# Depthwise convolution on TensorE: four taps per product instead of two, with the shifted copies issued by ScalarE, the diagonals built by VectorE, and a reworked opening

## The chip, the cores and the metric

One Trainium2 chip, one of its cores. The metric is the device time of one execution in microseconds (us). TensorE is the matrix engine (PE in the profile), VectorE is DVE, ScalarE is ACT, GpSimd is POOL, and SyncE is SP, which here only issues transfers and waits. Everything is float32. Most matrix products are made as three products of float32r halves (a high part and the rest), which keep float32 precision.

## The reference

Input x has 512 tokens of 1024 features. A first block has two layers: a pool mixer (mean over the last 2, 4, 8 or 16 tokens, minus the token, times a small matrix) and sliding-window attention, each with an RMS norm before it and a gated feed-forward behind it (2816 wide, with a 3-tap convolution over time). A second block follows:

```python
def conformer_conv(x, w_in, b_in, conv_w, conv_b, ln_g, ln_b, w_out, b_out):
    a, g = jnp.split(x @ w_in + b_in, 2, axis=-1)
    h = a * jax.nn.sigmoid(g)
    h = conv_general_dilated(h, conv_w, padding=30 on the left, groups=1024) + conv_b   # 31 taps
    h = jax.nn.silu(layer_norm(h, ln_g, ln_b))
    return h @ w_out + b_out
x = x + conformer_conv(rms_norm(x), ...)
x = x + square(relu(rms_norm(x) @ w1)) @ w2          # 4096 wide
```

The change touches the pool mixer (the opening), the first pair of each feed-forward, and the 31-tap convolution.

## The kernel before, in words

Features lie on the 128 partitions, in `C` = 8 chunks; tokens are the 512 columns. Every engine has its own program, and they wait on semaphores. Weights come in units of 128 x 1024 through four slots: SP loads `raw`, ScalarE copies the high part to `whi` (`split_hi`), VectorE subtracts it into `wlo` (`split_lo`), and TensorE runs a chain of 8 x 3 products (`three`, L594 to L596). A slot of `raw` is loaded again once it has been split.

*The opening.* The pool weights are scaled by the norm's gain (`weigh_pooled`, one half each on ScalarE and VectorE), `project_pooled` multiplies x with them (L683), `token_sums` adds the squares, and `window_mean` (L706, L709) applies the windows as banded matrices: a product with zeros opens each PSUM bank, and four products of 129 to 143 columns add into it. The bands (`near`, L530 and L533) are made by GpSimd from the identity in the constants `cst`, then weighted by VectorE (`mix`) and by both engines with 1/rms (`mixed`). `bias_residual` (ScalarE, L1079) adds the pool bias to `res`; `add_pooled` (L1530) and `prepare` (L958, L1347) then make the first feed-forward's inputs `xh` and `xl`, whose products begin in `first_chains`.

*The convolution stage.* For each chunk c the `ain` weights are applied (two chains), `gated` (VectorE, L1730) writes `hc` with 30 zero columns ahead of its 512, and the 31 taps of the chunk are shared out by hand:

- `PE_TAPS[c]` taps on TensorE (`convolve`, L867). SP copies `hc` into `shifted` (`shift_hc`, L480): partitions 0 to 63 hold 64 channels, 64 to 127 the same channels one token later, so one product of 128 rows with a two-diagonal matrix `dg` does two taps of 64 channels. There are two such column groups. ScalarE makes `dg` by scaling an identity (`diagonals`, L1230).
- `POOL_TAPS[c]` taps as ScalarE's scaled copies (`products`, L1244) which GpSimd adds up (L580).
- The others on VectorE (`own_tap`, L1686 and L1689, in the same step; `late_tap`, L1699, one step later, into the PSUM bank of `convolve`, so after `conv_done`). `collect` (L1707, L1712) adds the three parts into `hv`.

For ten units of `ain` and four of `aout` the low part is made otherwise: ScalarE writes the negated high part (`negate_high`, L1253) and a transfer issued by GpSimd adds the weights to it (L568). `statistics` (L877, L879) sums `hv` and its square over the features in two column groups; the layer norm and the output projection follow.

The order in every queue is fixed by the code. SP's is: two weight loads, then the four copies of a chunk, which wait for that chunk's `hc`.

Of the kernel before, what the change touches and what calls it, by code (L numbers as in the profile page):

```python
# [28 lines left out]
P = 128  # L29
D = 1024  # L30
T = 512
# [20 lines left out]
LAST_DIAGS = 5  # L52
HC = 3
LAST_GATED = 14
LOW_AT = {6: (0, 8), 7: (0, 10), 8: (1, 5), 9: (1, 7), 10: (2, 5), 11: (2, 7), 12: (3, 6), 13: (3, 8), 14: (4, 6),
          15: (4, 8), 16: (5, 7), 17: (7, 3), 18: (7, 6), 19: (7, 6)}
# [3 lines left out]
WARM = 10  # L60
# [105 lines left out]
def build(nc, xT, vec_in, cst_in, w_in, out):  # L166
# [3 lines left out]
    with ExitStack() as ctx:  # L170
# [14 lines left out]
        with ExitStack() as own:  # L185
# [3 lines left out]
            near = sb("near", [P, 5, PAD + P + PAD], F32, own)  # L189
            mix = sb("mix", [P, 2, 4, P + PAD], F32, own)  # L190
            mixed = sb("mixed", [P, NBLK, 4, P + PAD], F32, own)
            zero = sb("zero", [P, T], F32R, own)
# [5 lines left out]
        with ExitStack() as own:  # L198
# [7 lines left out]
            pair_w = sb("pair_w", [P, SHIFTS, C * TAPS], F32, own)  # L206
            pair_id = sb("pair_id", [P, GROUP], F32, own)
# [3 lines left out]
        with ExitStack() as own:  # L211
            hv = sb("hv", [P, C, T], F32, own)
            hc = sb("hc", [P, HC, TAPS - 1 + T], F32, own)
            dg = sb("dg", [P, DIAGS, max(PE_TAPS) // SHIFTS, SHIFTS, GROUP], F32, own)
            tapped = sb("tapped", [P, PARTS, T], F32, own)
            shifted = sb("shifted", [P, 2, SHIFTS, max(PE_TAPS) - SHIFTS + T], F32, own)
# [50 lines left out]
        near_steps = sem("near_steps")  # L267
        mix_steps = sem("mix_steps")
# [99 lines left out]
        on = slice(PAD, PAD + P + PAD)  # L368

# [59 lines left out]
        def _(sp):  # L429
# [31 lines left out]
            def load_pairs():  # L461

                w, i = VEC["conv_w"], CST_ID
                for s in range(SHIFTS):
                    rows = slice(s * GROUP, (s + 1) * GROUP)
                    sp.dma_start(pair_id[rows, :], cst_in[0:GROUP, i:i + GROUP]).then_inc(pairs_loaded, 16)
                    for g in range(SHIFTS):
                        n = C * TAPS - s
                        sp.dma_start(pair_w[rows, g, 0:n], vec_in[g * GROUP:(g + 1) * GROUP, w + s:w + s + n])\
                            .then_inc(pairs_loaded, 16)  # L470

            def shift_hc(c):

                n = PE_TAPS[c] - SHIFTS + T
                sp.wait_ge(hc_ready, c + 2)
                if c >= 2:
                    sp.wait_ge(conv_done, c - 1)
                for g in range(SHIFTS):
                    for s in range(SHIFTS):
                        sp.dma_start(shifted[s * GROUP:(s + 1) * GROUP, c % 2, g, 0:n],  # L480
                                     hc[g * GROUP:(g + 1) * GROUP, c % HC, s:s + n]).then_inc(hc_shifted[c % 2], 16)

            def load_conv_stage():

                ain, aout = ph["ain"], ph["aout"]
                shifts = {2 * c + KT - 2: c for c in range(C)}
                for n in range(ain.units + aout.units):
                    p, e = (ain, n) if n < ain.units else (aout, n - ain.units)
                    load(p, e // SLOTS, e % SLOTS)
                    if n in shifts:  # L490
                        shift_hc(shifts[n])

            for p in order:
                if p.name == "ffn0_up0":
                    sp.wait_ge(x_in[3], 16)
                if p.name == "pool":
                    load(p, 0, 0)
                    sp.dma_start(res[:, 0:2, 2 * P:T], xT[:, 0:2, 2 * P:T]).then_inc(x_in[0], 16)
                    for k in range(1, SLOTS):
                        load(p, 0, k)  # L500
                    continue
# [17 lines left out]
        def _(pool):  # L519


            pool.wait_ge(setup, 1)
            pool.wait_ge(cst_loaded, 16)
# [6 lines left out]
            nc.gpsimd.tensor_copy(near[:, 0, PAD:PAD + P], ident).then_inc(near_steps, 1)  # L530
            for g in range(4):
                pool.wait_ge(near_steps, g + 2)
                nc.gpsimd.tensor_tensor(near[:, g + 1, on], near[:, g, on],  # L533
# [1365 lines left out]
```

## Time and profile before

| | |
|---|---|
| median of 3 runs | 1448.52 us (1448.52 to 1449.33) |
| profiled execution, its own time | 1448.29 us |
| its span, first to last instruction | 1446.5 us |
| granted TensorE clock over the span | 1.00 |
| instructions in the trace | 19954 |

A span is counted from the first instruction. Line numbers are those of the kernel before. A row of the timeline merges neighbouring instructions of one kind and begins with its start and its length in us; in brackets stands the engine's idle time before it and what ended that. A float32 product is two records in the trace, a float32r product one.

### The profile page before, as it was taken

The page shows a single profiled execution, that of the slowest core. Times are in us where ns is not written, and L with a number is a line of the kernel's source. Part 1 is how long each engine was busy: PE and PEld are TensorE (multiplying, and loading weights), DVE is VectorE, ACT ScalarE, POOL GpSimd, SP SyncE. Part 2 cuts the span into 40 slices and gives each one's busy share as a digit, 9 for nine tenths or more (in the row PEclk, how much of TensorE's full clock was granted, in tenths as well). Part 3 has the DMA queues.
Part 4 walks back from the last instruction along what each step waited for, and adds up shares of the span by engine and source line. Part 5 has one row for each costly group of instructions (what it writes and reads, how often), then busy time and mean ns, then how long its engine had stood idle before and what let it go on. Part 6 is the DMA issues. An engine that isn't in the chain of part 4 may idle for free.

```text
span 1446.5 us, 19954 instructions
## 1 busy us (share of the span) xinstructions
PE 1437.2 (99%) x6828; PEld 1172.1 (81%) x6828; DVE 921.2 (64%) x1339; ACT 637.3 (44%) x994; POOL 204.8 (14%) x162
## 2 busy tenths in 40 slices
PE   9999999999999999999999999999999999999999
PEld 8788888888887898888888888766588888888887
DVE  7877773573645667777754755899988653544532
ACT  7444442342546675444422434798754321222210
POOL 4000000000302232000000003599511000000000
PEclk9999999999999999999999999999999999999999
DMA  5223223222322112232232232387613332222321
GB/s 191 88 99 104 87 102 116 73 102 91 121 90 71 30 60 81 96 108 94 91 125 75 88 108 81 101 186 179 161 45 102 116 101 89 100 102 88 102 94 51
DMA packets 44413, 144.34 MB, mean 100 GB/s; under 512 B 5184, under 2 KB 6208, under 8 KB 44352
## 3 DMA queue, kind: packets, MB, share of 16 engines
q1 hardware_dynamic: 41200, 133.79, 28.0%
q0 software_dynamic: 2016, 7.34, 2.8%
q10 hardware_dynamic: 1136, 2.42, 0.4%
q8 instruction: 35, 0.57, 0.2%
q14 instruction: 26, 0.21, 0.0%
HBM read 137.19 MB, written 2.10 MB: 96 GB/s over the span
## 4 chain that ended last, share of the span: by engine, by line
PE 94%; DVE 2%; ACT 1%; DMA 1%; issue 1%; POOL 1%; SPq 0%; ACTq 0%; DVEq 0%; POOLq 0%
PE bank L594 29%; PE bank L595 29%; PE bank L596 29%; PE bank L867 2%; PE bank L742 1%; PE bank L770 1%; PE bank L755 1%; DVE bank L1689 1%; PE bank L877 0%; DMA cst<-cst_in 0%; DMA shifted<-hc 0%; PE bank L922 0%; PE bank L923 0%; PE bank L635 0%; PE bank L926 0%
## 5 line engine op out<-in xcount | busy, mean ns | idle before, releaser
L594 PE MATMUL bank<-xh,whi 128*128 128x512 f32 x1184 | 464.9, 393 | 0.8 <-DVE wlo L1340 0.6
L596 PE MATMUL bank<-xh,wlo 128*128 128x512 f32 x1184 | 460.9, 389 | 0.0
L595 PE MATMUL bank<-xl,whi 128*128 128x512 f32 x1184 | 460.8, 389 | 0.0
L945 ACT ACTIVATE whi<-raw 128x1024 fp32r<-128x1024 f32 x244 | 255.8, 1050 | 238.7 <-PE bank L596 236.0
L1340 DVE TENSOR_TENSOR wlo<-raw,whi 128x1024 fp32r<-128x1024 f32 x230 | 288.0, 1252 | 43.8 <-ACT whi L945 35.9
L594 PEld LDWEIGHTS bank<-xh,whi 128*128 128x128 f32 x1184 | 222.2, 188 | 55.4 <-issue 7.1
L595 PEld LDWEIGHTS bank<-xl,whi 128*128 128x128 f32 x1184 | 222.3, 188 | 46.6 <-issue 1.2
L596 PEld LDWEIGHTS bank<-xh,wlo 128*128 128x128 f32 x1184 | 222.3, 188 | 46.4
L594 PE MATMUL bank<-ahi,whi 128*128 128x512 f32 x608 | 236.5, 389 | 0.0
L595 PE MATMUL bank<-alo,whi 128*128 128x512 f32 x608 | 236.5, 389 | 0.0
L596 PE MATMUL bank<-ahi,wlo 128*128 128x512 f32 x608 | 236.5, 389 | 0.0
L1361 DVE TENSOR_TENSOR res<-bank,res 128x512 f32 (+1 forms) x80 | 55.3, 691 | 202.6 <-PE bank L596 202.6
L545 POOL TENSOR_TENSOR ssum<-ssum,sq 128x512 f32<-128x512 f32 x32 | 47.7, 1490 | 733.8 <-ACT sq L965 403.2
L1412 DVE SCALAR_TENSOR_TENSOR tmp<-u,vec,tmp 128x512 f32<-128x512 f32 x176 | 124.2, 747 | 31.8 <-ACT tmp L1004 31.8
L596 PEld LDWEIGHTS bank<-ahi,wlo 128*128 128x128 f32 x608 | 114.1, 188 | 23.8
L594 PEld LDWEIGHTS bank<-ahi,whi 128*128 128x128 f32 x608 | 114.1, 188 | 23.7
L595 PEld LDWEIGHTS bank<-alo,whi 128*128 128x128 f32 x608 | 114.1, 188 | 23.5
L1004 ACT ACTIVATE tmp<-u,vec 128x512 f32<-128x512 f32 x88 | 71.6, 814 | 125.3 <-DVE u L1407 125.3
L1407 DVE TENSOR_TENSOR u<-bank,rinv 128x512 f32<-128x512 f32 x88 | 59.5, 685 | 63.8 <-PE bank L596 63.8
L580 POOL TENSOR_TENSOR prod<-prod,tapped 128x512 f32<-128x512 f32 x56 | 77.3, 1380 | 7.0 <-POOL prod L580 0.5
L1026 ACT ACTIVATE ahi<-tmp 128x512 f32 (+1 forms) x32 | 20.2, 632 | 121.6 <-DVE tmp L1437 121.6
L1008 ACT ACTIVATE gate<-tmp 128x512 f32<-128x512 f32 x44 | 27.9, 633 | 96.3 <-DVE tmp L1412 96.3
(191 smaller groups left out, 1344.6 us busy)
## 6 DMA issues: line engine op xcount, KB each, us to landing
raw<-w_ffn_up SPq DMA_DIRECT2D x88, 512.0 KB, 3.3
raw<-w_ffn_down SPq DMA_DIRECT2D x32, 512.0 KB, 3.2
raw<-w_mlp_up SPq DMA_DIRECT2D x32, 512.0 KB, 3.2
raw<-w_mlp_down SPq DMA_DIRECT2D x32, 512.0 KB, 3.2
raw<-w_ain SPq DMA_DIRECT2D x16, 512.0 KB, 3.4
raw<-w_ffn_down SPq DMA_DIRECT2D x16, 384.0 KB, 3.0
raw<-w_qkv SPq DMA_DIRECT2D x12, 512.0 KB, 3.2
wlo<-w_ain POOLq DMA_DIRECT2D x10, 512.0 KB, 7.3
```

The lines of the kernel that those rows point to most:

```text
L545: nc.gpsimd.tensor_tensor(ssum[:, which, :], ssum[:, which, :], x, ALU.add)\
L580: nc.gpsimd.tensor_tensor(prod[:, c % 2, :], a, tapped[:, (made + k) % PARTS, :], ALU.add)\
L594: nc.tensor.matmul(out_, hi, mh, start=first, stop=False)
L595: nc.tensor.matmul(out_, hi, ml, start=False, stop=False)
L596: return nc.tensor.matmul(out_, lo, mh, start=False, stop=last)
L867: mm = nc.tensor.matmul(bank[6 + b][g * GROUP:(g + 1) * GROUP, :], dg[:, c % DIAGS, q, g, :], shifted[:, b, g, SHIFTS * q:SHIFTS * q + T], ...
L945: nc.scalar.activation(whi[:, s, 0:tiles * P], raw[:, s, 0:tiles * P], ACT.Copy)\
L1004: nc.scalar.activation(tmp[:, k, :], u[:, k, 2:2 + T], ACT.Identity, scale=col(vec, par + 2), bias=col(vec, par + 3))\
L1340: V.tensor_tensor(wlo[:, s, 0:tiles * P], raw[:, s, 0:tiles * P], whi[:, s, 0:tiles * P].bitcast(F32), ALU.subtract).then_inc(lo_done, 1)
L1361: V.tensor_tensor(row(res, c), acc[k][:], row(res, c), ALU.add).then_inc(acc_free, 1)
L1407: V.tensor_tensor(u[:, k, 2:2 + T], acc[k][:], rinv[:], ALU.mult).then_inc(acc_free, 1)
L1412: V.scalar_tensor_tensor(tmp[:, k, :], u[:, k, shift:shift + T], col(vec, par + 4 * j + shift), tmp[:, k, :], op0=ALU.mult, op1=ALU.add).t ...
```

## The change

- `convolve` works with `SHIFTS[c]` taps per product: four for chunks 0 to 6 (four column groups of 32 channels, each row group of `shifted` one token later), two for chunk 7. `PE_TAPS` goes from 68 taps in all to 86, `POOL_TAPS` from 72 to 65, and VectorE's from 108 to 97. `DIAGS` (buffers of `dg`) goes from 3 to 2.
- `shift_hc` moves from SP to ScalarE, ahead of the chunk's `products`. Each of its transfers (one per column group) reads the overlapping windows of its channels and writes all 128 partitions. It is four transfers a chunk, as before, each with twice the rows (two for chunk 7).
- `diagonals` moves from ScalarE, 68 small copies, to VectorE, one product of two broadcast operands per chunk, behind `gated`. `load_pairs` brings its operands in 22 transfers, before 6.
- In step 6 the last `gated` comes after `collect`, no longer between taps.
- `statistics` uses four column groups of 32, each over half of the tokens.
- The opening: no product with zeros; `near` is made by GpSimd from ones with a memset and six selects, with no wait for `cst`; the residual bias goes to GpSimd; 8 warm-up products, before 10; the orders of splits and of the window weights change; x's last quarter and the tail of `vec` are issued by SP.
- The first pair of a feed-forward: ScalarE's and VectorE's second weight split come ahead of the taps.

```diff
-PE_TAPS = (8, 6, 6, 4, 6, 6, 14, 18)
-SHIFTS = 2
-GROUP = P // SHIFTS
+PE_TAPS = (8, 8, 8, 8, 8, 12, 20, 14)
+SHIFTS = (4, 4, 4, 4, 4, 4, 4, 2)
+GROUP = tuple(P // s for s in SHIFTS)
+ROUNDS = tuple(n // s for n, s in zip(PE_TAPS, SHIFTS))
-DIAGS = 3
-POOL_TAPS = (11, 10, 9, 9, 9, 9, 8, 7)
-LATE_TAPS = (0, 6, 8, 11, 11, 12, 4, 0)
-LATE_START = (2, 2, 2, 0, 0, 0, 0, 4)
+DIAGS = 2
+POOL_TAPS = (10, 9, 9, 8, 8, 8, 7, 6)
+LATE_TAPS = (2, 4, 6, 9, 12, 9, 0, 0)
+LATE_START = (2, 2, 2, 0, 0, 0, 0, 0)
-WARM = 10
+WARM = 8
...
-            def shift_hc(c):
-
-                n = PE_TAPS[c] - SHIFTS + T
-                sp.wait_ge(hc_ready, c + 2)
-                if c >= 2:
-                    sp.wait_ge(conv_done, c - 1)
-                for g in range(SHIFTS):
-                    for s in range(SHIFTS):
-                        sp.dma_start(shifted[s * GROUP:(s + 1) * GROUP, c % 2, g, 0:n],
-                                     hc[g * GROUP:(g + 1) * GROUP, c % HC, s:s + n]).then_inc(hc_shifted[c % 2], 16)
+                for shifts, (lo, hi) in SPREAD.items():
+                    group, n = P // shifts, PAIR_TAPS[shifts]
...
+                    for s in range(shifts):
+                        for g in range(shifts):
+                            src = vec_in[g * group:(g + 1) * group, w:w + C * TAPS].rearrange("p (c k) -> p c k", c=C)
+                            sp.dma_start(pair_w[shifts][s:P:shifts, g], src[:, lo:hi, s:s + n]).then_inc(pairs_loaded, 16)
...
+            def band(g, in_, base, sign, op):
+
+                nc.gpsimd.affine_select(near[:, g, :], near[:, in_, :], [[sign, P + PAD]], op, 0.0, base=base,
+                                        channel_multiplier=-sign).then_inc(near_steps, 1)
+
+            nc.gpsimd.memset(near[:, 4, :], 1.0).then_inc(near_steps, 1)
+            pool.wait_ge(near_steps, 1)
+            band(0, 4, 0, 1, ALU.is_equal)
+            band(3, 4, 0, 1, ALU.is_ge)
+            pool.wait_ge(near_steps, 3)
+            for g in (1, 2, 4, 3):
+                band(g, 3, WINDOWS[g - 1] - 1, -1, ALU.is_ge)
...
+            pool.wait_ge(setup, 2)
+            pool.wait_ge(squared, C)
+            for c in range(C):
+                pool.wait_ge(chain_done, 2 * (c // 2) + 2)
+                nc.gpsimd.tensor_scalar(res[:, c, :], res[:, c, :], col(pbs, c), None, ALU.add).then_inc(res_biased, 1)
...
-                nc.tensor.matmul(bank[BAND_BANKS[c]][:], zero[:, 0:P], zero[:], start=True, stop=False)
...
+                for q in range(ROUNDS[c]):
+                    for g in range(SHIFTS[c]):
+                        rows, at = slice(g * group, (g + 1) * group), SHIFTS[c] * q
+                        mm = nc.tensor.matmul(bank[6 + b][rows, :], dg[:, c % DIAGS, q, rows],
+                                              shifted[:, b, g, at:at + T],
+                                              start=(q == 0), stop=(q == ROUNDS[c] - 1))
...
-                nc.tensor.matmul(norm[0][0:GROUP, :], ones[:, 0:GROUP], hv[:, c, :],
-                                 start=(c == 0), stop=(c == C - 1))
-                nc.tensor.matmul(norm[0][GROUP:P, :], ones[:, 0:GROUP], sq[:, c % 2, :],
-                                 start=(c == 0), stop=(c == C - 1)).then_inc(stats_done, 1)
+                for j, x in enumerate((hv[:, c, :], sq[:, c % 2, :])):
+                    for h in range(2):
+                        rows, at = slice((2 * j + h) * QUADRANT, (2 * j + h + 1) * QUADRANT), slice(h * T // 2, (h + 1) * T // 2)
+                        mm = nc.tensor.matmul(norm[0][rows, at], ones[:, 0:QUADRANT], x[:, at],
+                                              start=(c == 0), stop=(c == C - 1))
...
+            def shift_hc(c):
+
+                n, group = PE_TAPS[c] - SHIFTS[c] + T, GROUP[c]
+                if c >= 2:
+                    act.wait_ge(conv_done, c - 1)
+                for g in range(SHIFTS[c]):
+                    window = hc[g * group:(g + 1) * group, c % HC, 0:n]
+                    taps = bass.AP(window.tensor, window.offset, [window.ap[0], (1, SHIFTS[c]), (1, n)])
+                    act.dma_start(shifted[:, c % 2, g, 0:n], taps).then_inc(hc_shifted[c % 2], 16)
...
                 act.wait_ge(hc_ready, c + 2)
+                shift_hc(c)
                 products(c, range(2))
...
+            def diagonals(c):
+
+                if c >= DIAGS:
+                    dve.wait_ge(conv_done, c - DIAGS + 1)
+                if c == 0:
+                    dve.wait_ge(pairs_loaded, 16 * sum(s * s + 1 for s in SPREAD))
+                shifts, rounds, group = SHIFTS[c], ROUNDS[c], GROUP[c]
+                shape = [P, rounds, shifts, group]
+                w = pair_w[shifts][:, :, c - SPREAD[shifts][0], 0:shifts * (rounds - 1) + 1:shifts]
+                V.tensor_tensor(dg[:, c % DIAGS, 0:rounds].rearrange("p q (g n) -> p q g n", g=shifts),
+                                pair_id[shifts][:].rearrange("p (q g n) -> p q g n", q=1, g=1).broadcast_to(shape),
+                                w.rearrange("p g (q n) -> p q g n", n=1).broadcast_to(shape), ALU.mult)\
+                    .then_inc(diag_ready, 1)
```

## Rows read from the trace of the kernel before

**Rows 1.** The page's first part: busy time and share of the span.

```profile
PE 1437.2 (99%) x6828; PEld 1172.1 (81%) x6828; DVE 921.2 (64%) x1339; ACT 637.3 (44%) x994; POOL 204.8 (14%) x162
```

**Rows 2.** Chain of waits, opening: start us, us, what.

```profile
2.23 6.83 DMA cst<-cst_in
...
14.74 0.77 POOL near L533
```

**Rows 3.** Timeline of the opening, TensorE and VectorE.

```profile
7.09 10.59 PE L683 MATMUL bank<-wg,res 128*128 128x256 f32 x48
...
21.94 0.50 PE L706 MATMUL bank<-zero 128*128 128x512 f32 x1
...
23.09 0.47 PE L706 MATMUL bank<-zero 128*128 128x512 f32 x1
...
37.02 0.19 PEld L594 LDWEIGHTS bank<-xh,whi 128*128 128x128 f32 x1 [0.62 <-DVE xl L1347]
...
41.24 2.30 DVE L1340 TENSOR_TENSOR wlo<-raw,whi 128x1024 fp32r<-128x1024 f32 x1
...
55.43 0.50 PE L594 MATMUL bank<-xh,whi 128*128 128x512 f32 x1 [0.62 <-DVE wlo L1340]
```

**Rows 4.** Chain of waits, convolution stage.

```profile
944.90 6.61 DMA shifted<-hc
951.55 2.80 PE bank L867 x12
...
965.46 2.73 PE bank L867 x12
...
980.14 1.87 PE bank L867 x8
...
1030.38 7.73 PE bank L867 x36
1038.11 0.42 PE bank L877
```

**Rows 5.** Timeline of VectorE, convolution stage.

```profile
929.43 0.75 DVE L1730 SCALAR_TENSOR_TENSOR hc<-bank,vec,gate 128x512 f32<-128x512 f32 x1 [0.19 <-ACT gate L1266]
...
942.33 0.75 DVE L1730 SCALAR_TENSOR_TENSOR hc<-bank,vec,gate 128x512 f32<-128x512 f32 x1
...
944.91 5.50 DVE L1689 SCALAR_TENSOR_TENSOR bank<-hc,vec,bank 128x512 f32<-128x512 f32 x7
...
959.57 0.75 DVE L1689 SCALAR_TENSOR_TENSOR bank<-hc,vec,bank 128x512 f32<-128x512 f32 x1
960.23 0.75 DVE L1699 SCALAR_TENSOR_TENSOR bank<-hc,vec,bank 128x512 f32<-128x512 f32 x1
...
974.74 0.69 DVE L1720 TENSOR_TENSOR tmp<-bank,rinv 128x512 f32<-128x512 f32 x1 [1.04 <-PE bank L596]
...
1039.97 3.34 DVE L1774 RECIPROCAL r<-r 128x512 f32<-128x512 f32 x1
```

**Rows 6.** Groups of VectorE, 925 to 1042: busy us, mean ns, idle before.

```profile
L1707 DVE TENSOR_TENSOR hv<-prod,hv 128x512 f32<-128x512 f32 x8 | 7.9, 993 | 0.4 <-POOL prod L580 0.4
```

**Rows 7.** The page's costliest groups, same columns.

```profile
L1340 DVE TENSOR_TENSOR wlo<-raw,whi 128x1024 fp32r<-128x1024 f32 x230 | 288.0, 1252 | 43.8 <-ACT whi L945 35.9
```

**Rows 8.** Groups of ScalarE, 925 to 1042.

```profile
L1244 ACT ACTIVATE tapped<-hc,vec 128x512 f32<-128x512 f32 x72 | 46.6, 720 | 7.8 <-DVE hc L1730 7.0 <-POOL prod L580 0.8
L1230 ACT ACTIVATE dg<-pair_id,pair_w 128x64 f32<-128x64 f32 x68 | 17.1, 335 | 0.0
```

**Rows 9.** Stretches: length, busy per engine, PEclk, DMA share, GB/s.

```profile
943.00:1013.00 70.00, 69.23 (x302) 46.90 (x301) 67.15 (x96) 62.26 (x111) 65.39 (x54) 1.00 0.79 189
1026.00:1030.00 4.00, 4.00 (x22) 1.35 (x20) 3.86 (x7) 4.00 (x8) 0.76 (x1) 1.00 0.56 135
```

**Rows 10.** The tile `shifted`: issue ns min/median/max, and landing.

```profile
L480 SPq DMA_DIRECT2D shifted<-hc x32: 467/597/2171, 930.2 to 1027.3; - x32
...
DMA to landing us min/median/max: 2.2/2.8/6.6
```

More of the change, by code:

```diff
@@ L529, in _ @@
             nc.gpsimd.tensor_tensor(square_of(0), square_of(0), square_of(2), ALU.add).then_inc(early_summed, 1)
[L530 to L533, printed above, removed]
-                                        near[:, g, PAD - (1 << g):2 * PAD + P - (1 << g)], ALU.add)\
-                    .then_inc(near_steps, 1)
+            pool.wait_ge(setup, 2)
[3 more added lines that the diff above has]
+                nc.gpsimd.tensor_scalar(res[:, c, :], res[:, c, :], col(pbs, c), None, ALU.add).then_inc(res_biased, 1)
             def add_squares(name):
@@ L997, in step @@
                             k = 2 * b + j
-                            split_hi(p.unit, i, k + AHEAD)
-                            if first and isinstance(i, int) and i == 0 and k == 0:
+                            opening = first and isinstance(i, int) and i == 0
+                            if not (opening and k == 1):
+                                split_hi(p.unit, i, k + AHEAD)
+                            if opening and k == 0:
                                 root(first)
+                                split_hi(p.unit, i, 1 + AHEAD)
                             par = VEC["glu"] + ((layer * FF_PAIRS + q0) * 2 + k) * 4 + 16 * i
@@ L1218, in _ @@
             p = ph["ain"]
-            def diagonals(c, part=0, parts=1):
-                if c >= DIAGS and part == 0:
-                    act.wait_ge(conv_done, c - DIAGS + 1)
-                if c == 0:
-                    act.wait_ge(pairs_loaded, 16 * SHIFTS * (SHIFTS + 1))
-                pairs = PE_TAPS[c] // SHIFTS
-                for q in range(part * pairs // parts, (part + 1) * pairs // parts):
-                    e = c * TAPS + SHIFTS * q
-                    for g in range(SHIFTS):
-                        last = nc.scalar.activation(dg[:, c % DIAGS, q, g, :], pair_id[:], ACT.Copy,
-                                                    scale=pair_w[:, g, e:e + 1])
-                if part == parts - 1:
-                    last.then_inc(diag_ready, 1)
             def products(c, ks):
@@ L1414, in step @@
                                                        op0=ALU.mult, op1=ALU.add).then_inc(done, 1)
-                        split_lo(p.unit, i, 2 * b + 1 + AHEAD)
+                        if not opening:
+                            split_lo(p.unit, i, 2 * b + 1 + AHEAD)
                         dve.wait_ge(gate_ready, pair + 1)
@@ L1531, in add_pooled @@
                                        op0=ALU.mult, op1=ALU.add).then_inc(pooled, 1)
-            for g in range(4):
-                weigh_pooled(g)
+            weigh_pooled(0)
+            window_weights()
+            weigh_pooled(1)
+            first_window_weights()
+            weigh_pooled(2)
+            weigh_pooled(3)
             evict_pooled(0)
@@ L1543, in _ @@
             V.tensor_tensor(square_of(4), square_of(4), square_of(0), ALU.add).then_inc(all_summed, 1)
[L1544 to L1545 removed]
+            for m in range(C):
+                for half in range(2):
+                    h = C * (m // REP) + REP * half + m % REP
+                    made = V.memset(qs[HD * half:HD * (half + 1), m:m + 1], HD ** -0.5 / SLOPE[h])
+            made.then_inc(q_scales, 1)
             dve.wait_ge(rms_ready, 1)
@@ L1756, in _ @@
                 gate_at = next((n for n in range(rounds) if issued[n] >= GATE_AT), rounds - 1)
-                gated_at = next((n for n in range(rounds) if issued[n] >= LAST_GATED), rounds - 1)
                 for n in range(rounds):
```

164 lines of the change are left out of this document (67 added, 97 removed).

## Prediction

> **What bounds the kernel now.** I read the page first. TensorE is busy for 99% of the span [rows 1], so only what shortens TensorE's queue, or a wait on it, can move the time. The chain of waits says where that is not so. In the opening it runs through the constant load, GpSimd's band matrices and ScalarE [rows 2], and in the convolution stage through one transfer of `shifted` [rows 4]. From 60 us to 916 us, and after the layer norm, TensorE is fed without gaps and the diff touches nothing there.
>
> The timeline of the opening [rows 3] shows TensorE working back to back: 48 records of projection from 7.09, the last 16 after the token sums, then eight window products from 21.94 at a pitch of about 1.15 (the second begins at 23.09). Two idle spots of 0.62 us follow, at 37.02 and 55.43.
>
> In the convolution stage the table of stretches [rows 9] has four engines nearly full over 70 us: TensorE 69.2, VectorE 67.2, GpSimd 65.4, ScalarE 62.3, and the DMA engines at 0.79. A step of this stage is one chunk of 128 channels. VectorE goes from its first `hc` at 929.43 to the reciprocal at 1039.97, 110 us, and waits in that time for little but TensorE, 1.04 us at 974.74 being the longest [rows 5]. So TensorE and VectorE end together, and taking work from TensorE alone gives nothing: the slower of the two sets the gain.
>
> **The opening, part by part.** *Zero products.* Each window product began with a 512-column float32r product of zeros. A float32r product of this width takes about 0.23 us of the queue (48 of them between 954.35 and 965.46 [rows 4]), and eight go: 8 x 0.22 = -1.7 us. *Start.* Ten warm-up products become eight and VectorE no longer waits for ScalarE's half of the pool weights. TensorE starts about 0.5 us earlier, but two fewer warm products may leave the first projection at the slower pace; bounds 0 and -0.5, I take -0.3. *Band matrices.* GpSimd makes them with seven operations before the constants land at 9.06, in place of five after [rows 2]. Selects do not occur in the trace; the nearest operation took 0.77 us, seven are 5.4 us, done before the first squares. Bounds: nothing, or, at twice that they end near 11 us and hold VectorE's second pool weight back by about 1.5 us. I take nothing. The 16 memsets of `q_scale` move into slack. *Residual bias.* Eight ScalarE operations go to GpSimd, which idled there, so ScalarE and VectorE can feed `xl` faster, two VectorE operations of 0.75 a chunk [rows 5] where TensorE needs 6 x 0.23 = 1.4. Of the 0.62 at 37.02 a part goes: -0.3. *First pair of the feed-forward.* A weight split moves ahead of the taps, and the 0.62 at 55.43 goes: -0.6. Against it, the split of unit 6 now comes after all eight `prepare` calls, and such a split took 2.30 us beside GpSimd's adds at 41.24 [rows 3]. It may be late by 0 to 0.8: +0.4. Sum: -1.7 - 0.3 - 0.3 - 0.6 + 0.4 = -2.5, bounds -3.3 and -0.5.
>
> **The convolution stage on TensorE.** A pair of taps was four records (two column groups, two passes). The chain has 7.73 us for 36 records and 1.87 for eight [rows 4]: 0.86 to 0.93 a pair, although the records last 0.6 each, so the two groups run side by side. There were 34 pairs. There are now 18 rounds of four groups and 7 of two, 25 in all. If four groups run side by side as two do, 9 rounds x 0.88 = -7.9 us. Statistics: two passes of 0.42 a chunk [rows 4] become four quadrants over half the columns, 0.42 in all: 8 x 0.43 = -3.4. Together -11.3. The dear end: if only two groups ran at once, a four-group round costs 1.75, and the stage gets 18 x 0.88 - 7.9 = +7.9 in place of -7.9. I take the cheap end, as two groups overlap fully in the rows.
>
> The Trainium skill bears on this (TensorE: Matmul & The Clock Gate, Part 3, table of measured speedups): three column tiles gave 2.38x and four row tiles 3.07x, not 3x and 4x. An estimate by that rule, 4 x 0.88 / 3.07 = 1.15 us a round, would make the TensorE saving smaller by 18 x 0.27 = 4.9 us. The trace has no four-group product.
>
> **The stage on VectorE.** Taps left to it fall from 108 to 97 (own 56 to 55, late 52 to 42). A tap that follows one on the same accumulator costs 5.50 / 7 = 0.786; one that alternates, 960.23 - 959.57 = 0.66 [rows 5]. Writing out the order gives 56 and 52 before, 59 and 38 after: 78.3 to 71.4, -6.9 us. Added are eight `diagonals`, 3200 columns in all. A split of 1024 columns takes 1252 ns [rows 7] and an evict of 512 some 0.69 [rows 5], so about 1.1 ns a column and 0.13 each, of which 0.08 lies over the operation before: +3.9. They have two SBUF inputs, like L1707, whose mean is 993 ns [rows 6] where the same width takes 0.69 when nothing stands in its way. Bounds 0 and 8 x 0.3 = 2.4; I take +1.2. Its waits for TensorE and GpSimd, about 1.7, go: -1.7. Sum: -6.9 + 3.9 + 1.2 - 1.7 = -3.5, bounds -4.7 and -2.3. The wait of `diagonals(c)` for `conv_done` of chunk c-2 is met a whole step earlier, so only two buffers cost nothing.
>
> **ScalarE and GpSimd.** ScalarE loses the 68 diagonal copies, 17.1 us, and 7 of 72 products, 4.5 us [rows 8]. It gains 30 DMA issues; on SP they took 597 ns each [rows 10], 18 us. Net -3.6. But the issues stand ahead of the products: at each chunk about 2.4 us in which ScalarE feeds GpSimd nothing. GpSimd has 7 of 64 adds fewer and catches up. Queued behind them are also the next sigmoid and two weight splits; by my ledger ScalarE finishes a step between 2 us before and 1 us after the next `hc`. I add nothing. SP is freed of the `hc` wait, and loads weights no later. 22 small pair loads (before: 6) take some 13 us of SP ahead of the attention weights; a slot is asked for when its last content is split, some three units of 5.5 us before the next is needed (two units fill 954.35 to 965.46 [rows 4]), which covers them.
>
> **The transfer.** Its bytes double: four transfers of 128 rows by 516 columns a chunk, where there were four of 64 rows. Before, the last of four landed 8.4 us after `hc` in a busy step (943.09 to 951.51 [rows 4, 5]), and single landings ranged from 2.2 to 6.6 [rows 10]. Chunk 7's four, alone on the engines, used a share of 0.56 over 4 us [rows 9], so each chunk adds 2.2 us of all 16. That makes about 10.5 us after `hc`. TensorE comes to the product 8 to 11 us after `hc`, so it waits 1 to 2 us at chunks 1 and 2 (it waited for the transfer at chunk 1 before too), then hardly. VectorE meets it at the first late tap, 13 us after `hc`, where 12.4 is the last landing that costs nothing. I take +0.5.
>
> **Sum.** Stage end: VectorE -3.5, transfers +0.5, and after the last `hv` one statistics chunk half as long, -0.4: -3.4. With the opening's -2.5: -5.9 us. The profiled execution took 1448.29 us around its span of 1446.5; it becomes 1442.4. The median of the runs shown is 1448.52, 0.2 higher, which makes 1442.6; I say 1442.5. What a measurement can tell from no change is about 0.2%, 2.9 us.
>
> **The rivals.** *TensorE sets the pace after all.* If `diagonals` meet no blocking and the tap counts let VectorE keep up, the stage gains up to TensorE's 11.3 less the wait at chunk 1, say 8, and the time is 1448.3 - 2.5 - 8 = 1438. Against it stands VectorE's ledger.
>
> *The transfer is late: the one that ends slower.* The table has the DMA engines at 0.79 over 70 us [rows 9], about 11.2 us of a 14.2 us step. With 2.2 more in a step of 13.2 they are at 1.01. If landings slip to H+15, where H is the chunk's `hc`, the late taps of four or five steps each start 2.6 us late: +11.7, that is 1448.3 - 5.9 + 11.7 = 1454. At H+13.7 the gain is gone. For it: the share itself, and that late taps begin with no delay from chunk 3 on. Against it: that share counts weight loads which are short when alone. The Trainium skill (DMA: Bandwidth & Descriptors, decision table) says transfers issued from different engines use the same 16 DMA engines, so moving the issue to ScalarE saves only issue time; it would speak for this rival.
>
> *Four groups do not run together.* TensorE's stage is then 7.9 - 3.4 = 4.5 us longer and it is the bound: 1448.3 - 2.5 + 4.5 = 1450. A half-way speedup would still leave TensorE level with VectorE, near 1444.
>
> *The stage does nothing.* Blocking and ScalarE's late products eat the 3.4, only the opening is left: 1446.
>
> **How the numbers follow.** Forecast (1440 to 1445) 0.55; TensorE pace, 1438, 0.15; stage does nothing, 1446, 0.15; late transfer 0.10; groups not together 0.05. Faster by over 0.2% (under 1445.6): 0.55 + 0.15 + a part of the third, 0.08 = 0.78. Slower: most of the late transfers, 0.07, and a little of the groups, 0.01 = 0.08. The same: 0.14. The range reaches from the TensorE pace to just above no change: 1437 to 1448.5; the forecast's own is 1440 to 1445.
>
> **What would show it.** Opening: no zero products, window pitch near 0.92, the first feed-forward product near 29 us and not 31.1, no wait at 55. Stage: eight records of L867 in four groups take about 0.9 a round; the span from first `hc` to the reciprocal is 107, not 110.5; the share of DMA above 0.9; `diagonals` of two rounds at 0.4 us, longer when beside a GpSimd add. I am wrong if L867 waits for `shifted` after chunk 2, if a four-group round takes over 1.1 us, or if ScalarE's products start later than 3 us after `hc`.

## The result, and the profile after

The changed kernel takes 1471.15 us (median of 4 runs, 1465.93 to 1472.09) where the kernel before took 1448.53 beside it: a ratio of 1.0144, with the interval 1.0132 to 1.0157. It is 22.6 us slower; 5.9 us faster was forecast, and the range ended at 1448.5. The profiled execution is the fastest of the four, 1465.93 us around a span of 1464.1, so 17.6 of the 22.6 us can be looked for in its trace.

The page's first part, and the rows of the 40 slices for TensorE's busy time and its clock:

```profile
PE 1432.6 (98%) x6884; PEld 1168.0 (80%) x6884; DVE 925.2 (63%) x1334; ACT 612.9 (42%) x911; POOL 209.9 (14%) x165
...
PE   9999999999999999999999999978899999999999
...
PEclk9999999999999999999999999989999999999999
```

TensorE is busy 4.6 us less than before [rows 1] and yet the span is 17.6 us longer: it now waits, and one slice of its clock falls. Both are in the convolution stage. The stretches of that stage (the same 70 us as in [rows 9], and the two worst steps in it; the last columns are granted clock, DMA share and GB/s):

```profile
943.00:1013.00 70.00, 54.58 (x268) 36.65 (x266) 55.03 (x76) 45.90 (x64) 52.71 (x45) 0.88 0.84 207
943.00:963.00 20.00, 9.09 (x40) 6.50 (x42) 16.98 (x23) 13.10 (x18) 16.30 (x15) 0.78 0.88 223
963.00:983.00 20.00, 20.00 (x100) 13.05 (x93) 13.64 (x19) 10.34 (x15) 13.97 (x12) 0.88 0.82 203
```

No engine is full any more: TensorE 54.6 of 70 us against 69.2, VectorE 55.0 against 67.2, ScalarE 45.9 against 62.3, while DMA went from 0.79 to 0.84. TensorE waits for something that no engine computes, and the others wait behind it. The tile `shifted` names it (issue in ns; then who waited for the tile, us and times; then the landings):

```profile
L1256 ACTq DMA_DIRECT2D shifted<-hc x30: 550/646/3471, 928.7 to 1041.8; - x30
...
  PE bank L869: 23.0, 4
  DVE bank L1689: 8.7, 2
  DVE hv L1716: 3.6, 1
...
DMA to landing us min/median/max: 3.7/7.5/15.5
```

Against [rows 10] the median landing went from 2.8 to 7.5 us and the longest from 6.6 to 15.5. TensorE waits 23.0 us in four places: 2.09 at chunk 0, 10.88 at chunk 1, 4.51 at chunk 4 and 5.54 at chunk 7. The largest, at chunk 1, on ScalarE and on TensorE (timeline):

```profile
942.08 1.06 ACT L1232 ACTIVATE wlo<-whi 128x1024 fp32r<-128x1024 f32 x1
943.04 1.04 ACT L950 ACTIVATE whi<-raw 128x1024 fp32r<-128x1024 f32 x1
944.12 1.07 ACT L1232 ACTIVATE wlo<-whi 128x1024 fp32r<-128x1024 f32 x1
944.12 6.13 ACTq L1256 DMA_DIRECT2D shifted<-hc  x4
950.30 5.71 ACT L1223 ACTIVATE tapped<-hc,vec 128x512 f32<-128x512 f32 x9 [5.12 <-issue]
...
951.05 0.39 PE L598 MATMUL bank<-xh,wlo 128*128 128x512 f32 x1
962.32 3.64 PE L869 MATMUL bank<-shifted,dg 128*32 128x512 f32 x16 [10.88 <-DMA shifted<-hc]
...
977.89 1.92 PE L869 MATMUL bank<-shifted,dg 128*32 128x512 f32 x16
...
1009.28 3.37 PE L869 MATMUL bank<-shifted,dg 128*32 128x512 f32 x16 [4.51 <-DMA shifted<-hc]
```

`hc` of chunk 1 was written at 941.87. ScalarE was still in the weight splits and negations of the step before, so the first copy was issued at 944.12; the four issues held ScalarE until 950.3; the product began at 962.32, 20.4 us after `hc`. Between the issues of the copies, two more kinds of transfer start (GpSimd's and SP's rows of the same timeline), GpSimd's accumulating weight transfers and SP's weight loads:

```profile
944.50 1.04 POOL L570 DMA_DIRECT2D wlo<-w_ain  x1
...
948.25 0.87 POOL L570 DMA_DIRECT2D wlo<-w_ain  x1
...
945.67 5.03 SPq L448 DMA_DIRECT2D raw<-w_ain  x3
```

The first two copies landed 3.8 and 7.8 us after their issue, the last two 13.7 and 15.5. The three weight loads (512 KB each) were issued before or within 0.8 us of the last copy, and landed after 12.8 to 15.2 us.

The 16 records at 962.32 take 3.64 us and the 16 at 1009.28, behind a wait of 4.51, take 3.37; the same 16 at 977.89, with no wait ahead, take 1.92. The granted clock stands at 0.78 in the 20 us up to 963: from 955 to 966 it is 0.50, so the clock fell while TensorE was idle, and it ran at the lower of its two levels (1.2 GHz) for some products behind that. That is a second cost of a wait, on top of the wait. Not every wait has it: with SP issuing (next section) the 16 records behind waits of 2.28 and 1.95 us took 1.93 and 1.92.

The opening, TensorE in the changed kernel, then the rows of the kernel before that answer to the last three:

```profile
6.20 7.17 PE L686 MATMUL bank<-wg,res 128*128 128x256 f32 x32 [1.10 <-DMA res<-xT]
14.25 3.69 PE L686 MATMUL bank<-wg,res 128*128 128x256 f32 x16 [0.87 <-DVE zT L1480]
...
22.23 7.47 PE L711 MATMUL bank<-mixed,zT 128*128 128x129 f32 x64
29.45 0.48 PE L596 MATMUL bank<-xh,whi 128*128 128x512 f32 x1
...
42.38 1.02 PE L637 MATMUL bank<-ssum,ones 128*128 128x512 f32 x2
...
918.83 1.88 PE L637 MATMUL bank<-ssum,ones 128*128 128x512 f32 x4
```

```profile
31.11 0.48 PE L594 MATMUL bank<-xh,whi 128*128 128x512 f32 x1
...
42.87 1.02 PE L635 MATMUL bank<-ssum,ones 128*128 128x512 f32 x2
...
920.29 1.88 PE L635 MATMUL bank<-ssum,ones 128*128 128x512 f32 x4
```

The eight windows take 7.47 us, 0.93 each where the pitch was 1.15 [rows 3], and the first feed-forward product comes 1.66 us earlier. By the token sums at 42.4 only 0.5 of that is left. There is no wait at 55 us any more, and at 919 the lead is 1.46 us.

### The profile page after: what moved, and what is told of

Its sections match the earlier page's. It is cut to its first block and busy times, and to the rows that moved or that the text cites. A ratio compares the mean times of both kernels' runs of the same rounds, so it can differ in the third digit from the quotient of the medians.

```text
span 1464.1 us, 19991 instructions
## 1 busy us (share of the span) xinstructions
PE 1432.6 (98%) x6884; PEld 1168.0 (80%) x6884; DVE 925.2 (63%) x1334; ACT 612.9 (42%) x911; POOL 209.9 (14%) x165
## 5 line engine op out<-in xcount | busy, mean ns | idle before, releaser
L582 POOL TENSOR_TENSOR prod<-prod,tapped 128x512 f32<-128x512 f32 x49 | 67.2, 1372 | 5.6
```

What stands on the lines that cost most here:

```text
L582: nc.gpsimd.tensor_tensor(prod[:, c % 2, :], a, tapped[:, (made + k) % PARTS, :], ALU.add)\
```

## Where the copies are issued

**Issued by SP, all else as changed.**

```diff
+                    if n in shifts:            # in SP's weight loop, the old place
+                        shift_hc(shifts[n])    # four overlapping copies, sp.dma_start
...
-                shift_hc(c)                    # on ScalarE, ahead of products
```

> The changed kernel with shift_hc back on SP, at the place where the kernel before had it (after two weight loads, waiting there for hc). Bytes, pattern and taps are those of the change. Theory 1 (the doubled bytes keep the DMA engines full, whoever issues): still slow, 1462 to 1472 us, single landings of shifted 7 to 12 us. Theory 2 (the place on ScalarE: behind two splits and two negations, and ScalarE held for 4 to 6 us by the issues): back to 1440 to 1446 us, landings up to 7 us. Both in part: 1450 to 1460 us.

Measured 1451.26 us, ratio 1.0016 (1.0006 to 1.0026). So 19.9 us of the 22.6 come with the place of the issue. The tile `shifted` in this version:

```profile
L484 SPq DMA_DIRECT2D shifted<-hc x30: 548/634/2844, 928.2 to 1029.1; - x30
...
  PE bank L883: 11.8, 4
...
DMA to landing us min/median/max: 3.6/5.3/11.6
```

It is still no gain: 11.8 us of waits stay. (Over 943 to 1013 the DMA engines' mean share is 0.95 in this version and 0.84 in the changed kernel, which is 20 us slower: the mean share alone does not say which copies are late.)

**Issued by ScalarE, but ahead of the last splits and negations of the step before** (two of each ahead of chunk 1, one of each for chunks 2 to 6).

```diff
+                    act.wait_ge(hc_ready, c + 3)
+                    shift_hc(c + 1)
                     for e in range(2 * (c + AHEAD) + (c > 0), ...):
                         split_hi(p.unit, 0, e)
                         negate_high(e)
```

> The changed kernel, ScalarE still issues the copies, but those of chunks 1 to 6 are issued ahead of the weight splits and negations that end the step before, as soon as hc is there. If it is the place in ScalarE's queue (first issue of chunk 1 was 2.3 us after hc, behind splits) that makes them late: waits for shifted fall by some 2 us a chunk, 1458-1466. If it is the issues' own length on a full queue and the bytes: 1469-1473, because issues still take 3 to 6 us and what stands behind them (now the next splits) is late by as much. If the held splits starve TensorE: slower than 1473.

Measured 1459.31, ratio 1.0074 (1.0057 to 1.0091): 11.8 us come back by position alone. ScalarE at chunk 1:

```profile
942.12 4.48 ACTq L1256 DMA_DIRECT2D shifted<-hc  x4
946.70 1.07 ACT L950 ACTIVATE whi<-raw 128x1024 fp32r<-128x1024 f32 x1 [5.40 <-PE bank L598]
947.80 1.06 ACT L1232 ACTIVATE wlo<-whi 128x1024 fp32r<-128x1024 f32 x1
```

The copies are issued at `hc` + 0, and the negation that GpSimd's first accumulating transfer needs comes behind them: GpSimd waits 4.4 us for it and issues at 949.18, where the changed kernel's was issued at 944.50, without a wait and behind GpSimd's own adds. The product of chunk 1 starts at 952.4, 10.3 us after `hc` and not 20.4. The position does two things at once, earlier copies and later weight transfers; this run does not part them.

**SP held at the old places without issuing.**

```diff
+                    if n in shifts:
+                        sp.wait_ge(hc_ready, shifts[n] + 2)
+                        if shifts[n] >= 2:
+                            sp.wait_ge(conv_done, shifts[n] - 1)
```

> The changed kernel with one thing put back: SP again waits for each chunk's hc at its old place in its queue before it goes on with weight loads, but issues no copy there; ScalarE still issues them. Weight loads running ahead are the cause (SP, no longer held by the hc wait, fills the DMA engines before the copies come): the waits for shifted shrink from 23 us towards the 12 us of the version with SP issuing, and the time falls from 1471 to about 1455-1460. The place on ScalarE is the cause (issues late, and ScalarE held during them): nothing here changes that, 1469-1473. A bad side effect (weight loads late): above 1474.

Measured 1469.02, ratio 1.0136 (1.0119 to 1.0153). So loads issued before `hc` are not the cause: at most some 2 us are theirs. But this run does not put the loads behind the copies. SP goes on as soon as `hc` is there, while ScalarE reaches the copies later and needs time to issue them; at chunk 1:

```profile
943.61 7.07 ACTq L1261 DMA_DIRECT2D shifted<-hc  x4
945.21 3.24 SPq L448 DMA_DIRECT2D raw<-w_ain  x2
```

At chunk 3 both loads (979.93 and 980.30) go out ahead of three of the four copies. With SP issuing, the same program order puts every load behind all four copies of its chunk (at chunk 1 the next load is issued at 945.95, the copies from 940.39). Loads that stand beside the copies, and not behind them, are therefore a rival that no run here tests.

## How much the traffic matters

**Seven eighths of the accumulating weight transfers left out**, once with ScalarE issuing and once with SP. Both kernels leave out most of the low part of 14 weight units.

```diff
-                nc.gpsimd.dma_start(wlo[:, e % SLOTS, :], weights, accum_op=ALU.add)
+                nc.gpsimd.dma_start(wlo[:, e % SLOTS, 0:P], weights[:, 0:P], accum_op=ALU.add)
```

> The changed kernel, where the accumulating weight transfers that GpSimd issues (14 units of 1024 columns) cover only the first 128 columns; left out are seven eighths of the low part of these units. Bytes and contention on the DMA engines are the cause: 14 x 0.9 MB of reads and writes less in the stage, copies land in about 4 us in place of 7.5, issues on ScalarE fall from 3-6 us a chunk to 2.5, and the time falls to 1450-1456. The place on ScalarE alone is the cause, whatever the traffic: above 1462.

Measured 1451.86, ratio 1.0021 (1.0012 to 1.0031): 19.3 us less.

> The changed kernel with SP issuing the copies at their old place (measured 1451.3) and the same seven eighths of the accumulating weight transfers left out. If the full DMA engines make the four waits for shifted (11.8 us): they shrink below 3 us and the time falls to 1441-1445, which is what the forecast wanted. If it is something else (the copy's own pattern, hc's place): stays at 1449-1451.

Measured 1445.09, ratio 0.9975 (0.9964 to 0.9987): 6.2 us less, and the only kernel with four taps in chunks 0 to 6 that is faster than before. The expectation had the waits below 3 us; 8.3 stay, 4.65 of them at chunk 7. First with ScalarE issuing, the tile `shifted` and the group of ScalarE's products; then with SP issuing, the 70 us stretch and the tile:

```profile
L1256 ACTq DMA_DIRECT2D shifted<-hc x30: 550/786/2905, 928.5 to 1032.5; - x30
...
DMA to landing us min/median/max: 3.7/4.8/10.0
```

```profile
L1223 ACT ACTIVATE tapped<-hc,vec 128x512 f32<-128x512 f32 x65 | 42.1, 721 | 33.3 <-issue 28.6 <-POOL prod L582 4.7
```

```profile
943.00:1013.00 70.00, 68.64 (x365) 48.62 (x364) 68.40 (x95) 51.32 (x72) 59.76 (x49) 1.00 0.67 162
```

```profile
  PE bank L883: 8.3, 3
DMA to landing us min/median/max: 3.4/4.9/5.9
```

The place cost 19.9 us with full traffic and costs 6.8 with light traffic. ScalarE is held by its issues as long as before the cut (28.6 us of idle ahead of the products against 28.4), so the holding alone is not what makes the 20 us: the cost of the place falls with the traffic and with the landings (median 7.5 to 4.8 us). Each of the two, place and traffic, is dearer with the other. Through which step is not shown. It is not that one version's copies meet accumulating transfers and the other's don't: at chunk 1 the first of those goes out 0.38 us after the first copy with ScalarE issuing and 0.04 us after it with SP. What differs there is the late start (2.3 us after `hc`), and the weight loads beside the copies.

## Half the bytes, and other forms of the copy

**Two taps per product everywhere**, with the tap counts of the kernel before; once from ScalarE and once from SP. Bytes as before the change, in two transfers a chunk; VectorE still builds the diagonals.

```diff
-PE_TAPS = (8, 8, 8, 8, 8, 12, 20, 14)
-SHIFTS = (4, 4, 4, 4, 4, 4, 4, 2)
+PE_TAPS = (8, 6, 6, 4, 6, 6, 14, 18)
+SHIFTS = (2, 2, 2, 2, 2, 2, 2, 2)
```

> The changed kernel's code with two taps per product for all chunks and the tap counts of before: half the bytes of shifted, two transfers a chunk of 128 rows each, still issued by ScalarE ahead of the products, diagonals still on VectorE, new opening. Theory 1 (bytes): 1445 to 1450 us, with landings of 3 to 6 us. Theory 2 (the place on ScalarE): still over 1455 us, since conv products wait behind late issues. Theory 3 (the overlapping reads of the same few partitions are slow per byte): landings near the changed kernel's, 6 to 10 us, although the bytes are half, and a time between.

Measured 1459.64, ratio 1.0070 (1.0053 to 1.0087).

> As the run with two taps issued by ScalarE (1459.6 us), but issued by SP in the place of before. What differs from the kernel before is the opening, the diagonals on VectorE, the shape of the transfers (two of 128 rows for four of 64), statistics in four groups and the last gated at the end of its step. Opening -1.5 us by the profile after, statistics up to -3.4 us on TensorE, diagonals +4 to +6 us on VectorE, which is nearly full: 1445 to 1452 us. If the place on ScalarE is the cause in this version too, the step from 1459.6 to here is 8 us or more; under theory 3 (overlapping reads slow per byte) landings are above 5 us.

Measured 1457.48, ratio 1.0062 (1.0045 to 1.0079). Here the place is worth 2 us; in this version ScalarE was ready at every `hc` and issued its first copy within 0.05 us of it, so this pair does not test a late issue. The second misses its expectation of 1445 to 1452. Both are slow for another reason: VectorE does all the taps of before and the diagonals as well. From the first `hc` to the seventh it takes 87.7 us (928.9 to 1016.6), the kernel before 83.4 (930.2 to 1013.5), and then 17.6 us more to the last `hc` where before it was 11.9. The group of the diagonals with SP issuing, and TensorE's one wait for a copy:

```profile
L1713 DVE TENSOR_TENSOR dg<-pair_id,pair_w 128x384 f32<-128x384 f32 (+4 forms) x8 | 8.9, 1113 | 0.3
...
1038.60 9.85 PE L883 MATMUL bank<-shifted,dg 128*64 128x512 f32 x36 [7.22 <-DMA shifted<-hc]
```

**The last `gated` back between the taps**, in this version and in the four-tap one.

```diff
+                    if n == gated_at and c == C - 2:
+                        gated(C - 1)
...
-                if c == C - 2:
-                    gated(C - 1)
```

> The changed kernel with two taps per product everywhere, SP issuing, as measured at 1457.5, and in addition the last gated of step 6 back between the taps (after 14 of them). If the late last gated is what exposes the end there (its product of chunk 7 waited 7.2 us for the copy and the last hc came 17.6 us after the one before): the wait at chunk 7 goes and the time falls by 6 to 9 us, to 1449-1451. If VectorE is simply overloaded by the diagonals: at most 2 us less, 1455.5-1457.5.

Measured 1454.79, ratio 1.0034 (1.0021 to 1.0047): 2.7 us less, not 6 to 9; the wait at chunk 7 fell from 7.22 to 4.56.

> The changed kernel with SP issuing (measured 1451.3) and the last gated back between the taps of step 6, after nine of them. There the wait at chunk 7 was 2.5 us and the step 13.4 us, so 1 to 3 us less: 1448.5-1450. If the copies of chunks 0 to 2 alone hold VectorE, the end moves with them: no change, 1451.

Measured 1454.43, ratio 1.0039 (1.0025 to 1.0053), against 1.0016 without it: no gain, if anything a loss. The wait at chunk 7 was 3.49 after 2.52. I had put the slow end of the two-tap versions down to the late `gated`; it explains 2.7 us of their 9. The trace offers the diagonals (8.9 us) and the copy's wait for the rest, but no run parts them.

**Two taps in chunks 0 to 2, four in 3 to 6**, SP issuing.

```diff
+PE_TAPS = (8, 6, 6, 8, 8, 12, 20, 14)
+SHIFTS = (2, 2, 2, 4, 4, 4, 4, 2)
+POOL_TAPS = (11, 10, 9, 8, 8, 8, 7, 6)
+LATE_TAPS = (1, 6, 7, 9, 12, 9, 0, 0)
```

> As the version before it, but chunks 0 to 2 with two taps per product and nearly the tap counts of the kernel before, four taps in chunks 3 to 6. If the doubled bytes matter only where weight loads crowd the engines (waits of 2.3, 5.1 and 2.0 us at chunks 0 to 2): these go, and with the four-tap savings later the time is 1445-1448. If the crowding just moves to the next four-tap chunks: 1449-1452.

Measured 1455.90, ratio 1.0051 (1.0035 to 1.0068), slower than either side of the expectation. (Of the waits that it names, the one of 2.0 us stood at chunk 4, not 2.) The waits of chunks 0 to 2 did go; there are 0.84 us at chunk 3, 2.41 at chunk 4 and 3.53 at chunk 7, and VectorE had more taps and larger diagonals (8.2 us) to do. So waits come where the wide copies are, but the time also holds VectorE's extra work, which this run does not part from them.

**Sixteen plain copies of 32 rows in place of four overlapping ones**, SP issuing.

> As the run with four taps issued by SP (1451.3 us), but each chunk's copies as sixteen plain transfers of 32 rows in place of four overlapping ones: the same bytes to the same places. Theory 3 (overlapping pattern slow): faster than the four on SP by 3 us or more. Otherwise, with the same landing of the last one plus the issue time, 16 x 0.6 = 9.6 us against 4 x 0.6 to 1.1, it is later by some 5 us a chunk: 1465 us or more.

```diff
+                for s in range(SHIFTS[c]):
+                    for g in range(SHIFTS[c]):
+                        sp.dma_start(shifted[s:P:SHIFTS[c], c % 2, g, 0:n],
+                                     hc[g * group:(g + 1) * group, c % HC, s:s + n])...
```

Measured 1464.52, ratio 1.0111 (1.0094 to 1.0128), 13 us slower than the overlapping form. Each lands sooner (median 2.7 us), but 116 issues at a median of 594 ns need 10 to 13 us of SP a chunk. The overlapping source is not slow; it saves issues.

**The kernel before, its own four 64-row copies issued by ScalarE.**

```diff
-                        sp.dma_start(shifted[s * GROUP:(s + 1) * GROUP, c % 2, g, 0:n], ...
+                        act.dma_start(shifted[s * GROUP:(s + 1) * GROUP, c % 2, g, 0:n], ...
```

> The kernel before with one thing changed: its own four 64-row copies a chunk are issued by ScalarE ahead of the products, not by SP. The place alone costs something even with half the bytes: ScalarE is held 4 issues x 0.6 us a chunk and also still makes the diagonals, so its queue of 62.3 us in 70 becomes 71 in 70; it becomes the bound and the time rises by 4 to 12 us, to 1453-1460. If the place costs only together with the doubled bytes, at most 2 us more: 1448.5-1450.5.

Measured 1458.17, ratio 1.0069 (1.0054 to 1.0084). ScalarE's groups:

```profile
L1231 ACT ACTIVATE tapped<-hc,vec 128x512 f32<-128x512 f32 x72 | 46.4, 720 | 18.5 <-issue 14.1 <-POOL prod L567 4.4
L1217 ACT ACTIVATE dg<-pair_id,pair_w 128x64 f32<-128x64 f32 x68 | 17.1, 334 | 0.0
```

The place alone, with nothing else changed, costs 9 us. ScalarE also still makes the diagonals here (17.1 us), so a part of the 9 may be its full queue. At chunk 1 the first copy goes out 2.9 us after `hc` and the product waits 5.05 us for it, where it waited 0.8 in the kernel before. Three weight loads went out between 944.6 and 945.6, ahead of the first copy; in the kernel before they came behind the fourth.

## The parts that do not copy

**Only the opening and the first feed-forward pair**, put on the kernel before. (Diff: the opening's part of the one shown.)

> The kernel before with only the opening and the first pair of the feed-forward of the change; the convolution stage is that of before. By the traces of the changed kernel the first hc ends 1.5 us earlier, so 1447.0. By the forecast (2.5 us): 1446.0. If an earlier opening is lost again in the loops between 60 and 916 us: 1448.5.

Measured 1447.16, ratio 0.9991 (0.9982 to 1.0000). Its first `hc` ends at 928.4, 1.8 us earlier.

**And the statistics in four quadrants.**

> The version with only the opening, and in addition the statistics in four column groups over half the tokens (chain step of 0.42 us in place of two). The stage on TensorE is 3.4 us shorter but VectorE keeps its work, so only the last chunk's tail is gained: 0.4 us, 1446.6. If TensorE was the true bound of the stage: 1443.7.

Measured 1446.27, ratio 0.9984 (0.9975 to 0.9993): 2.3 us faster than before by the ratio. No kernel that computes the whole reference was measurably better.

**And four taps in chunk 7 alone**, SP issuing. The first of the two writes the copies of chunks 0 to 6 in another order of rows than the weights have, so those taps are mixed; the second has them in order.

```diff
+PE_TAPS = (8, 6, 6, 4, 6, 6, 14, 20)
+SHIFTS = (2, 2, 2, 2, 2, 2, 2, 4)
```

> The previous version, and in addition four taps per product in chunk 7 alone, 20 taps on TensorE in place of 18 and so two taps fewer on VectorE; the copies are issued by SP and only this chunk's bytes double, at the end, where the DMA engines were at 0.56. Its product falls from 9 rounds of two groups (7.7 us) to 5 rounds of four (4.4 us), and it stood at the end of the chain. If the landing of the wider copy (some 5 us in place of 2.4) is covered, 3 us less: 1443.5. If the landing is what the product then waits for: 1445 to 1446.5.

> The version with opening and quadrant statistics, and chunk 7 alone with four taps per product, rows of all copies interleaved as the weights are. The same work in time as the version labelled last_chunk_four, where the wider copy landed 4.9 us after its last issue and the product waited 2.8 us for it at half the granted clock: 1446.2 again, no gain from the shorter product. If the destination order of the rows matters for the copies of chunks 0 to 6: 1447-1450.

Measured 1446.23, ratio 0.9985 (0.9976 to 0.9994), and 1447.29, ratio 0.9983 (0.9973 to 0.9992). TensorE in the second, and its stretches:

```profile
1032.23 6.20 PE L890 MATMUL bank<-shifted,dg 128*32 128x512 f32 x40 [3.74 <-DMA shifted<-hc]
```

```profile
1028.00:1032.00 4.00, 0.49 (x8) 0.01 (x2) 3.86 (x6) 3.97 (x6) 3.65 (x3) 1.00 0.81 218
1032.00:1039.00 7.00, 6.77 (x56) 2.08 (x56) 4.57 (x7) 5.39 (x7) 6.71 (x7) 0.76 0.93 236
```

The product is five rounds of four groups; the same 40 records took 4.50 us at chunk 6 in the version with SP issuing. Here it waited 3.74 us and then ran at a granted clock of 0.76, 6.20 us. What the wider product saves, the wider copy takes.

## Why the prediction was wrong

**The transfer and its place (forecast +0.5 and "I add nothing").** This is the step that failed. The forecast had the last copy land 10.5 us after `hc`: 8.4 as before, and 2.2 for the added bytes. In the trace it was 20.4 at chunk 1. At the same chunk it was 14.3 with SP issuing, 10.2 with ScalarE issuing ahead of the splits, 14.9 with ScalarE and light traffic, and 8.6 with SP and light traffic. So with SP issuing and little beside them the wide copies stay inside the term; what it left out is the place and what else is under way. Three things were missing. First, the issues start late: I wrote that ScalarE finishes a step between 2 us before and 1 us after the next `hc`, and at chunk 1 it was 2.3 after. Second, I costed an issue at 0.6 us from the narrow copies [rows 10]; four wide ones take 4.4 us even at chunk 0 with no other transfer under way, and all of the changed kernel's took 30.7 us, not 18. Third, I let the copies pay for their own bytes only, as if the share of 0.79 [rows 9] left room in every microsecond. At chunks 1 and 2 they stand beside accumulating transfers that landed after 9.0 to 12.8 us and beside SP's weight loads that landed after 8 to 15.2; the mean share is 1.04 from 953 to 968. How much of the 20 us each of the three makes is not parted. The rival "the transfer is late" named the mechanism, late landings on full DMA engines, but not the place; it had landings at `hc` + 15, a price of 1454 and a chance of 0.10. With SP issuing, that rival is about what happened (1451.3). With ScalarE issuing the place adds 19.9. Two of the three signs of being wrong came: L869 waited for `shifted` at chunks 4 and 7, and ScalarE's products of chunk 1 began 8.4 us after `hc`. The rule of the Trainium skill that I weighed there (DMA: Bandwidth & Descriptors, Rules for kernel authors), that transfers issued from different engines run on the same 16 DMA engines, is in keeping with the runs: less traffic on GpSimd's queue made the copies on ScalarE's land sooner (median 4.8 us for 7.5).

**The clock (not priced).** L869 is busy 29.5 us for its 172 records in the changed kernel and 24.5 us for the same 172 with SP and light traffic, by the groups of TensorE: 5 us in these products alone, most of it behind the waits of chunks 0, 1 and 4, where the clock had fallen. A forecast that lets a wait in must add this.

**Four groups run together (forecast: 0.88 a round).** Right. Two rounds take 1.92 us at 977.89, and the rival of two at a time falls. The estimate by the Trainium skill's table (TensorE: Matmul & The Clock Gate, Part 3), 1.15 us a round, is not borne out for these products: 0.93 (24 records in 2.78 us) to 0.96.

**TensorE's and VectorE's stage.** TensorE's queue was shorter (busy 4.6 us less, with the slow products in it), and that was worth nothing, as it waited 23.0. VectorE's taps cost what was read (0.65 to 0.79 each). The diagonals were busy 8.0 us in all, where the forecast's numbers make 4.6, or 5.8 with blocking:

```profile
928.75 0.43 DVE L1700 TENSOR_TENSOR dg<-pair_id,pair_w 128x256 f32<-128x256 f32 x1
941.91 1.50 DVE L1700 TENSOR_TENSOR dg<-pair_id,pair_w 128x256 f32<-128x256 f32 x1
...
1041.21 2.03 DVE L1700 TENSOR_TENSOR dg<-pair_id,pair_w 128x896 f32<-128x896 f32 x1
```

The same 256 columns take 0.43 or 1.50, the latter beside a GpSimd add.

**The opening (forecast -2.5).** Mis-sized by 1 us. The zero products gave their 1.7, but TensorE then waited 1.10 us for x and 0.87 for the evicted projection, and most of what was left at 29.45 was lost while VectorE fed `xl` at its pace: the 0.62 at 37 became a gap of some 0.2 at each of several chunks. The 0.62 at 55 did go. The weight load of unit 6 waited 0.54 us for its split, and TensorE lost nothing by it: the unit's second product is again 0.5 us earlier than before.

**What stays open.** The four-tap kernel with SP issuing is 8.8 us above the forecast. 6.2 go with the accumulating transfers and 1.0 is the opening; about 1.6 is not assigned. Whether, on ScalarE, late copies, accumulating transfers or the weight loads beside the copies do most of the harm was not parted.

## What to carry to other kernels

Before a transfer is moved to another engine's queue, write down when that queue reaches it, and which transfers of other queues can then start beside it that used to stand behind it: here the same copies cost 20 us more on ScalarE than on SP, and 12 of the 20 came back when they stood ahead of the last weight splits. Price a copy that stands on the critical path by its landing under the traffic of its own microseconds, not by an average share, and add to each wait of TensorE the time at the lower clock that follows it. When a kernel has several engines nearly full, a saving on one of them that is bought with bytes can cost more than it gives: here TensorE's shorter queue was paid for in waits for the copies.

## What the runs showed of the hardware

- Issuing a copy of 128 rows by 516 columns held its engine 1.1 us on average at chunk 0 (four in 4.41 us), and up to 3.47 us on ScalarE in the changed kernel (4.40 in the version with SP held) and 2.84 us on SP. The median of 646 ns hides it.
- The copy's landing with the same bytes and the same pattern was 4.9 us (median, at most 5.9) with the accumulating transfers cut and SP issuing, and 7.5 us, up to 15.5, in the changed kernel.
- Four column groups of 32 run side by side: 0.96 us a round at full clock, which makes 0.24 us for a product of 512 columns in two passes.
- The statistics in four quadrants of 256 columns take 0.64 us for eight records, at the end of the chain; the two column groups of the kernel before took 1.08 (four records of 512 columns).
- A VectorE product of 256 columns with two SBUF inputs ranged from 0.43 to 1.50 us; the long one ran beside a GpSimd add.
